# A two-block transformer kernel: in the hybrid attention the bias is added by VectorE, with four buffers for p, scores four units ahead, and head pairs without a break between them

## The reference, cut to what matters

```
def compress(k, pos, w1, w2):
    blocks = jnp.concatenate([chunks[:, :-1], chunks[:, 1:]], axis=2)
    blocks = blocks + pos[None, None, :, None, :]
    flat = jnp.moveaxis(blocks, 3, 2).reshape(B, blocks.shape[1], G, CMP_LEN * Dh)
    return jax.nn.gelu(flat @ w1) @ w2
...
lg_c = jnp.einsum('bqghd,bcgd->bghqc', qa, kc_c) * scale
p_cmp = masked_softmax(lg_c + token_bias(bias_a, dist_c), dist_c >= 0)
...
lg_w = jnp.einsum('bqghd,blgd->bghql', qa, kwin) * scale
p_w = masked_softmax(lg_w + token_bias(bias_a, dist_w), valid_w)
...
o_a = g[..., 0:1] * o_cmp + g[..., 1:2] * o_slc + g[..., 2:3] * o_win
...
lg_b = jnp.where(valid_b, lg_b + token_bias(bias_b, dist_b), NEG)
m = jnp.maximum(lg_b.max(axis=-1, keepdims=True), sink)
e = jnp.exp(lg_b - m)
p_b = e / (e.sum(axis=-1, keepdims=True) + jnp.exp(sink - m))
```

## Time and profile before

| | |
|---|---|
| median of 3 runs | 3555.34 us (3554.73 to 3558.83) |
| profiled execution | 3552.92 us |
| its span | 3551.2 us |
| mean granted TensorE clock | 0.904 |
| busy shares of the span | PE 83%, PEld 50%, DVE 43%, ACT 13%, POOL 25% |

### The profile page before, as it was taken

How to read it: one execution, slowest core, us unless ns; L and a number is a source line. 1 busy time by engine, 2 the same in 40 slices (tenths; PEclk the granted TensorE clock), 3 DMA queues, 4 the chain that set the end, 5 groups by cost and what they waited for, 6 DMA issues and landing times.

```text
span 3551.2 us, 26444 instructions
## 1 busy us (share of the span) xinstructions
PE 2939.1 (83%) x9622; PEld 1773.2 (50%) x9622; DVE 1510.8 (43%) x2314; ACT 448.9 (13%) x1004; POOL 875.0 (25%) x633
## 2 busy tenths in 40 slices
PE   5999887899999999999998899477776666666666
PEld 3444656488888884444468756233332222222222
DVE  5664454122200010001015512866666767767765
ACT  1000332111101010001004411100010000100000
POOL 2110100000000000000000001554555656566663
PEclk9999887999999999999978899788888888788888
DMA  9998310455544444444620034999999999999998
GB/s 380 395 401 326 97 48 1 152 204 201 196 150 150 153 149 147 154 152 148 206 92 1 0 116 166 417 382 417 381 404 422 422 422 421 408 422 422 421 422 357
DMA packets 228264, 916.44 MB, mean 258 GB/s; under 512 B 17804, under 2 KB 33364, under 8 KB 156244
## 3 DMA queue, kind: packets, MB, share of 16 engines
q0 software_dynamic: 99840, 637.57, 43.7%
q1 hardware_dynamic: 128069, 277.67, 23.0%
q10 hardware_dynamic: 272, 0.13, 0.0%
HBM read 912.12 MB, written 2.15 MB: 257 GB/s over the span
## 4 chain that ended last, share of the span: by engine, by line
PE 59%; DMA 23%; DVE 10%; POOL 4%; issue 2%; ACT 2%; DVEq 0%; POOLq 0%; SPq 0%; ACTq 0%
PE ps L1213 17%; DMA arena<-in_peer_v,proj 11%; PE ps L901 11%; PE ps L1239 9%; PE ps L1428 6%; DMA proj<-in_peer_u,proj 4%; DMA ring<-in_w_in 3%; DMA proj<-in_peer_v,proj 3%; PE ps L1022 3%; POOL arena L483 2%; PE ps L939 2%; PE ps L1405 2%; DMA arena<-in_w_mod 2%; PE ps L1302 1%; POOL proj L483 1%
## 5 line engine op out<-in xcount | busy, mean ns | idle before, releaser
L1428 PE MATMUL ps<-proj,gates 128*128 128x512 f32 x992 | 570.1, 738 | 393.1 <-DMA proj<-in_peer_v,proj 273.1
L1213 PE MATMUL ps<-hT,ring 128*128 128x256 f32 x2816 | 608.2, 379 | 1.5 <-ACT hT L522 1.5
L1428 PEld LDWEIGHTS ps<-proj,gates 128*128 128x128 f32 x992 | 230.9, 241 | 729.1 <-issue 601.7
L1213 PEld LDWEIGHTS ps<-hT,ring 128*128 128x128 f32 x2816 | 535.4, 190 | 74.5 <-issue 2.2
L483 POOL DMA_INDIRECT proj<-in_peer_u,proj x128 | 201.9, 1577 | 1475.0 <-DVE proj L2015 1310.6
L901 PE MATMUL ps<-ring,hT 128*128 128x512 f32 (+2 forms) x960 | 382.2, 559 | 9.9 <-DMA ring<-in_w_in 9.9
L2022 DVE CUSTOM_DVE_ANT_0 arena<-arena,yT 128x2048 f32<-128x2048 f32 x128 | 291.5, 2291 | 211.0 <-DMA arena<-in_peer_u,proj 210.4
L2022 DVE CUSTOM_DVE_ANT_0 proj<-proj,yT 128x2048 f32<-128x2048 f32 x128 | 292.2, 2292 | 127.1 <-DMA proj<-in_peer_u,proj 123.4
L1239 PE MATMUL ps<-ring,arena 128*128 128x512 f32 x704 | 304.1, 595 | 2.7 <-ACT arena L721 2.7
L901 PEld LDWEIGHTS ps<-ring,hT 128*128 128x128 f32 x960 | 176.1, 195 | 215.7 <-issue 192.3
L1428 PE MATMUL ps<-arena,gates 128*128 128x512 f32 x512 | 235.5, 603 | 43.9 <-DMA arena<-in_peer_v,proj 43.8
(11 more groups left out here) (415 smaller groups left out, 2704.3 us busy)
## 6 DMA issues: line engine op xcount, KB each, us to landing
arena<-in_w_mod POOLq DMA_DIRECT2D x96, 1024.0 KB, 12.4
ring<-in_w_in SPq DMA_DIRECT2D x52, 1024.0 KB, 12.2
ring<-in_ffn_w_gate SPq DMA_DIRECT2D x44, 1024.0 KB, 5.2
ring<-in_ffn_w_up SPq DMA_DIRECT2D x44, 1024.0 KB, 5.2
ring<-in_ffn_w_down SPq DMA_DIRECT2D x44, 1024.0 KB, 4.8
ring<-in_w_out SPq DMA_DIRECT2D x32, 1024.0 KB, 5.2
ring<-in_peer_wq SPq DMA_DIRECT2D x16, 1024.0 KB, 10.6
ring<-in_w_in SPq DMA_DIRECT2D x16, 960.0 KB, 17.2
```

The lines of the kernel that those rows point to most:

```text
L1213: ins = pe.matmul(ps[:, 4 * m + f, 0:T], ring[:, s, k, P * f:P * (f + 1)], hT[:, KS * s + k, :], start=(s == 0 and k == 0), stop=(s == SLO ...
L1428: ins = pe.matmul(ps[:, 4 * t + b, :], diag[:, j, :], row_slots[n % ROWS][:, NB * b:NB * (b + 1)], start=(h == 0 and j == 0), stop=(h == H ...
```

## The change

- **Bias.** The table is kept negated. The bias load reads a second DRAM table, `bias_shifted`, in which each of the 32 rows stands 128 times; the SP queue makes it by one DRAM-to-DRAM transfer in the first block, ahead of the fifth `w_out` load. The partitions now come in plain order. `score` has only the matmul of queries and keys. In `row_max` VectorE forms bias minus score in place in PSUM with one SCALAR_TENSOR_TENSOR, takes the minimum, and exp runs with scale -1.
- **Buffers and order.** `p` has four buffers (in the memory of `w1`); scores run four units ahead, row_max three, exp two.
- **Queries.** They are turned into the free upper halves of banks 4 and 5, in units 2 and 3.
- **Pairs.** There is one run over all eight pairs. VectorE loops over six; TensorE has two loops of two, with straight code between. values of a pair's last unit is issued in the next pair, and its copy into yT after row_max of unit 4.
- **Positions** are added by VectorE as it copies `xk`; L1275, L1902 and gelu's bias go.

More of the change, by code:

```diff
@@ L754, in softmax_exp, with q_out, turned_out @@
             for h in range(2):
-                ins = act.activation(hyb["p"][:, u % 2, h, 0:n], ps[:, u % 4, T * h:T * h + n], ACT.Exp, bias=hst["max"][:, u % NU, h:h + 1],
+                ins = act.activation(hyb["p"][:, u % 4, h, 0:n], ps[:, u % 4, T * h:T * h + n], ACT.Exp, bias=hst["least"][:, u % NU, h:h + 1], scale=-1.0,
                                      accum_out=hst["sum"][:, u % NU, h:h + 1])
             ins.then_inc(sem("att_exp"), 1)
[L759 to L762, removed]
+        def q_out(k):
+            for h in range(2):
+                r = slice(DK * h, DK * (h + 1))
+                ins = act.activation(hyb["q"][r, k, h, :], ps[r, 4 + k, T:2 * T], ACT.Copy, scale=DK ** -0.5)
+            ins.then_inc(sem("q_out"), 1)
+        def turned_out(i, past, u, more):
+            t, br = UNITS[u]
+            act.wait_ge(*at("att_turned", at_unit(i, past, u + 2)))
+            if more and u in (2, 3):
+                q_out(u - 2)
+            if past or u >= 2:
+                act.wait_ge(*at("att_pv", at_unit(i, past, u)))
             r, n = {"cmp": ((7, 15)[t], 2)}.get(br, (P, 2 * (t + 1)))
@@ L1310, in turn_p @@
+        def turn_p(i, past, u, more):
+            t, br = UNITS[u]
+            if past or u >= 2:
+                pe.wait_ge(*at("att_pT", at_unit(i, past, u)))
+            if more and u in (2, 3):
+                if u == 2:
+                    pe.wait_ge(*at("q_in", i + (past + 2)))
+                turn_q(u - 2)
+            pe.wait_ge(*at("att_p", at_unit(i, past, u + 1)))
             for h in range(2):
@@ L1923, in weigh @@
-        def weigh(i, g, u):
-            t, br = UNITS[u % NU]
+            vec.wait_ge(*at("att_score", at_unit(i, past, u + 1)))
+            m = hst["least"][:, u % NU, :]
+            off = P * (1 - t)
+            cols = slice(off + 31, T, 16) if br == "cmp" else slice(off, off + n)
+            bias = hyb["bias"][:, bass.ds(i * 2 + (2 * (past + u // NU) + (16 if br == "ban" else 0)), 2), cols]
+            scores = ps[:, u % 4, :].rearrange("p (h k) -> p h k", h=2)[:, :, 0:n]
+            link(vec.scalar_tensor_tensor(out=scores, in0=scores, scalar=-1.0, in1=bias, op0=ALU.mult, op1=ALU.add))
@@ new lines, in head_pair @@
+                if u == 1 and past:
+                    attended(i, past - 1, 1, NU - 1)
+            attended(i, past, 0, NU - 2)
+        vec.wait_ge(*at("bias_in", 16))
+        q_in(0, 0)
+        for u in range(3):
+            row_max(0, 0, u)
+        head_pair(0, 0)
+        with vec.Fori(0, 6) as i:
+            link.begin(i, vec_chain=NU + 2 * nb + NU + nb + (NU - nb), att_max=NU, att_p=NU, q_in=1, att_out=2)
+            head_pair(i, 1)
+        link.end(6)
+        head_pair(0, 7, False)
@@ L1966, in _ @@
+        attended(0, 7, 1, NU - 1)
         residual_add(BLK["out2"], EVB["out2"], None)
```

178 lines of the change are left out of this document (82 added, 96 removed).

## The result

| | before | after |
|---|---|---|
| median of 4 runs | 3555.03 us (3552.62 to 3558.83) | 3505.78 us (3502.05 to 3509.32) |
| profiled execution | 3552.92 us | 3509.27 us |
| its span, mean granted clock | 3551.2 us, 0.904 | 3507.5 us, 0.903 |

The ratio is 0.986, with a 95% interval of 0.9843 to 0.9877. Forecast were 3502 us and a range of 3486 to 3526.

What follows compares the result with a forecast made beforehand. TensorE was taken to bound the attention stage, VectorE after the change. Profiled 3552.9 less 13.1 (positions) and 40.1 (stage), transfers 0, gave 3499.7; with the median 2.4 above, 3502 us, 80% range 3486 to 3526.

Steps and rivals of the forecast that it cites:

- Which engine sets the pace: Attention stage: TensorE, the bound before, loses 12.5 us of matmuls a pair at full clock; VectorE then sets the pace.
- VectorE's chain, 18.0 a pair: Attention pair: VectorE's weights 6.96, minima 3.96, new instruction 3.96, sink 1.0 and copies with branch 2.1 sum to 18.0 us.
- the term of 2.1: Part of VectorE's time per attention pair: query copies 0.76, two yT copies 2 x 0.52, loop branch 0.3 us.
- The pair-end wait, 0.7: Pair's end: VectorE waits 0.7 us for values while TensorE does four transposes and four value instructions; loop pair 18.7 us.
- the reserve: Attention stage: 2 us added to 150.2, giving 152, for stretches at half clock in which VectorE must wait.
- The rival of a partly fallen clock: Attention stage: TensorE's clock falls for half the time, bursts cost 1 to 3 us a pair, total 3510 to 3526; chance 0.09.
- PSUM in and out at half rate: Rival on VectorE's new instruction: PSUM read and write take turns, +3.7 us a pair, +29, total 3531; chance 0.10.
- The transfers: SP queue: the 6.3 MB DRAM-to-DRAM copy takes 25 or 49 us, about 87 are available; cost 0, bias load unchanged.
- Positions, -13.1: Compress stage: position rows added in VectorE's copies instead of 64 one-column instructions; -13.1 us, bounds -12 to -16.
- the 0.5 for query copies and lost overlap: Compress stage: some 0.3 us more for four query copies replacing two, and 0.2 for lost overlap.
- the 0.2 behind the groups: Compress stage: 0.2 us added after the two matmul groups of 4.9 and 6.84 us to reach the new end, 1844.6.
- own range: Total time 3488 to 3516 from the terms' bounds, without the rivals; the 80% range was wider, 3486 to 3526.

## Why the prediction was right

**Which engine sets the pace: right.** TensorE lost its half of the score instructions and VectorE's chain took over. Twice over the experiments show it: taking 2.16 us of VectorE's steps away, with 2.6 us more for TensorE, shortened the pair by 2.3, and giving TensorE 4.8 us more lengthened it by 0.7.

**VectorE's chain, 18.0 a pair: 0.3 short.** Measured is 19.67 less the wait of 1.34, or 18.33. Products, minima, weights and the new instruction cost what was forecast (0.72 and 0.46 start to start, with the address steps hidden behind the product). Short was the term of 2.1 for query copies, yT copies and branch: the queries' copy shows 0.35 us of address steps, the pair's end 0.55, and together these came to 2.57 (0.92, 0.68 and 0.97); the other terms were a little less than forecast. The queries' copy and the copy into yT in mid-pair:

```profile
1918.07 0.50 DVE L1963 COPY proj<-proj 128x256 f32 x2 [0.35 <-DVE vrows L1941]
...
1921.21 0.42 DVE L1968 COPY yT<-ps 128x256 f32 x1 [0.24 <-DVE vrows L1943]
```

**The pair-end wait, 0.7: measured 1.34.** The mechanism was right, its size not. I took 0.11 for each value matmul, but those of the compressed unit take 0.16, and I left out 0.14 us of scores. The four transposes take 0.56 where 0.43 stood in the sum. VectorE's cover was 0.3, not the 0.5 of the sum: the unit's two steps partly run under the product.

**The clock: right in the main, with the reserve used up.** Behind its first units the stage saw the clock fall four times. Three of these, of 3 to 4 us each, left the pair at 19.67: TensorE had room. The fourth lasted 10.2 us (1880.60 to 1890.80 shows 0.52) and made its pair 21.59 from copy to copy, 1.9 more than the others: VectorE waited 0.7 us for scores and, before its copy at the pair's end, 2.34 instead of 1.34 for values. The kernel without the DRAM copy shows the same, a pair of 21.52 at a mean clock of 0.76. TensorE's rows ahead of the fall and in it:

```profile
1878.45 0.41 PE L1326 MATMUL ps<-tab,proj 128*128 128x128 f32 x2 [1.38 <-DVE proj L1958]
...
1881.09 0.59 PE L1326 MATMUL ps<-tab,proj 128*7 128x128 f32 x2 [1.16 <-DVE proj L1958]
1881.47 1.06 PE L1348 MATMUL ps<-arena 128*128 128x128 f32 x4
1882.33 1.91 PE L1305 MATMUL ps<-hT 128*128 128x256 f32 x4
```

Two gaps of over a microsecond stand within 3 us. The clock is 1.00 up to 1880.2 and 0.50 (1.2 GHz) from 1880.3, inside the second gap. But the pair from 1915.47 to 1935.14 has such gaps at the same two places of the program, and up to 1.43 us elsewhere, at a granted clock of 1.00 throughout:

```profile
1919.78 0.41 PE L1326 MATMUL ps<-tab,proj 128*128 128x128 f32 x2 [1.04 <-DVE proj L1958]
...
1922.41 0.39 PE L1326 MATMUL ps<-tab,proj 128*7 128x128 f32 x2 [1.16 <-DVE proj L1958]
```

So the gaps alone don't tell when it falls; that stays open. In the six versions with some or all of the bias on TensorE and the new order, the clock never falls again from the first copy into yT to the stage's end. The rival of a partly fallen clock wanted 1 to 3 us on every pair and a total from 3510; it came on one pair, for 1.9 us in all, and the reserve of 2 held that. That the two sizes agree is luck: nothing in the prediction derives the 2. The rival's price was also mis-added: 12.5 x 1.5 = 18.8 is half of the work at 1.2 GHz; with half of the time there it is 12.5 / 0.75 = 16.7. The Trainium skill, "TensorE: Matmul & The Clock Gate", section "A second HAM failure mode: psum-queue depth-cycling", tells of a kernel whose short idles between groups of matmuls make the clock swing. The clock did swing here, with four falls, but whole pairs with such idles kept 1.00, and the changed kernel's mean in the stage is 0.91, against 0.86 before.

**PSUM in and out at half rate: fell**, 695 ns against 691 for a reduce. By the Trainium skill, "VectorE: DVE Perf Modes", section "The perf-mode tier table (the rule you actually need)", two-operand work and reduces with a PSUM operand run at the single rate, as a float32 two-operand instruction in SBUF does; the trace agrees (691 ns for a reduce from PSUM, 692 for the product in SBUF). The three-operand form, 695 ns, costs the same here.

**The transfers: right.** The copy took 27.5 us where 25 or 49 were forecast, and out1 ran its fifth unit without a wait. TensorE's row of the changed kernel holds four units, the third to the sixth, 64 instructions, and no idle:

```profile
501.55 27.63 PE L1028 MATMUL ps<-ring,yT 128*128 128x512 f32 x64
```

**Positions, -13.1: measured -12.0.** The additions were right: L1280 starts 6.77 us after the transposes, against 6.38 before, the 0.4 of the sum. Wrong was the clock. I gave the first group of L1280 the 4.9 us of the earlier trace rows, which had part of its time at full clock (a mean of 0.72 from 1832.3 to 1837.1). In the changed kernel both groups ran at 1.2 GHz, 13.83 us in one piece:

```profile
1826.46 4.50 PE L1273 MATMUL ps<-tab,yT 128*128 128x128 f32 x20 [2.66 <-DVE yT L1899]
1833.23 13.83 PE L1280 MATMUL ps<-hT,proj 128*128 128x30 f32 x64 [2.27 <-DVE hT L1915]
```

In the ten other versions with this part the same group took from 12.12 to 13.84 us, in five of them 13.83 or 13.84: which part of it meets the full clock changes from execution to execution. The group cost 2.1 us more than the 11.74 of the sum. That the whole missed by only 1.1 is because the 0.5 for query copies and lost overlap and the 0.2 behind the groups weren't needed, and 0.2 more went; errors of two signs, not a better sum.

**The sum.** Six pairs longer by 0.97 are 5.8, the slow pair 1.9, and first and last pair with fill and drain 0.3 (38.3, forecast were 38.0). Less the reserve, 1.8 between the unrounded 150.2 and 152, that is the 6.2 us by which the stage missed. With 1.1 from the positions and 2.3 up and down the program, the profiled execution came out 9.6 above its sum of 3499.7, and the median 3.8 above 3502. The median is nearer by luck: I put it 2.4 above the profiled execution, as before, and it lies 3.5 below. The lower end of the own range, 3488, isn't the sum of its terms either: 2.9 on part 1, 1.8 and 2 below 3502 give 3495.

**What the prediction didn't ask:** whether the bias had to move at all. TensorE's own length with the bias is 18.05 us a pair, VectorE's with it 18.33, without it about 14.4 (less the 3.96 of the new instruction). The old pair's 23.9 was the order's doing, and the low clock's that came with it. The forecast rested on the 12.5 us that TensorE kept, and never priced a kernel that is only reordered; measured, that one gets all of the gain: 3502.0 against 3505.8.

## What to carry to other kernels

Work out the chain of each engine for the new version, not only for the one that is relieved: where both come out near each other (18.05 and 18.33 here), moving work between them gains nothing, and sharing it by shape until the two chains meet gains most (16.3). A wait on the engine that sets the pace is worth nearly its full length (1.20 of 1.34 us here) and is cheaply removed by moving the waiting instruction behind work that is ready; the same move was worth half where the other engine was the bound. Estimate a pair-end wait by listing everything that the other engine issues between the release and the result, in its order, with the durations of those very shapes.

## What was not expected of the hardware

- Value matmuls over 7 or 15 partitions take 0.16 us start to start, the same with 128 partitions 0.11: fewer partitions are no cheaper, and here dearer. Why, no run shows.
- A fall to 1.2 GHz can be free: from 1941.8 to 1945.0 TensorE ran at 0.50, and the pair took 19.67 us, as the one at 1.00.
- A transfer of 6.3 MB from DRAM to DRAM in rows of 1.5 KB took 27.5 us, 229 GB/s, not much below the bias load of 4.2 MB in 16.1 us.
- Address steps of VectorE cost nothing behind a product that isn't waited for, and 0.24 to 0.35 us before a copy that stands behind an instruction it waits for.
